# Two-block transformer kernel: compressed scores against zero-padded keys of two heads, and fewer, larger visits of small products between the dense ones

## The reference, cut to what matters

```python
# first block: the index score of query block i, over 8 index heads
s_h = jnp.einsum('bqhd,bsd->bqhs', iqb, ikf) * idx_scale            # 64-long dot products
score = jnp.einsum('bqh,bqhs->bqs', iwb * w_scale, jax.nn.relu(s_h))
...
# second block: keys and values are compressed, 31 blocks of 32 tokens each, for 2 groups of heads
def compress(t, pe, w1, w2):
    tb = t[:, blk] + pe[:, None, :]
    tb = jnp.moveaxis(tb, 3, 2).reshape(B, n_cmp, G, CMP_BLOCK * D)  # 2048 long
    return jax.nn.gelu(tb @ w1) @ w2                                 # w1: 2048 x 256, w2: 256 x 64
k_cmp = partial_rope(rms_norm(compress(kc, pe_k, w1_k, w2_k), k_gains[0]), cmp_end)
v_cmp = compress(vc, pe_v, w1_v, w2_v)
s_cmp = jnp.einsum('bsghd,bngd->bghsn', q, k_cmp)                    # compressed scores, 8 heads, 64 long
p_cmp = masked_softmax(s_cmp, cmp_end[None, :] <= pos[:, None])
```

## Time and profile before

| | |
|---|---|
| median of 3 runs | 1563.77 us (1563.75 to 1566.7) |
| the profiled execution, its own time | 1567.3 us |
| its span in the profile | 1565.5 us |
| PE (TensorE products) busy | 1540.6 us, 98% of the span, 8659 instructions |
| PEld (weight loads) busy | 1248.5 us, 80% |
| DVE busy | 875.1 us, 56% |
| ACT busy | 609.3 us, 39% |
| chain that ended last | 90% PE, 6% DVE, 2% ACT |

### The profile page before, as it was taken

One profiled execution on the slowest core, in us unless ns is written; L12 is line 12 of the kernel. 1 busy time (PEld: TensorE's weight loads), 2 busy tenths in 40 slices (PEclk: granted clock), 3 DMA queues, 4 the chain that ended last, 5 costly groups with the idle time before them and its releaser, 6 DMA issues.

```text
span 1565.5 us, 21012 instructions
## 1 busy us (share of the span) xinstructions
PE 1540.6 (98%) x8659; PEld 1248.5 (80%) x8659; DVE 875.1 (56%) x1589; ACT 609.3 (39%) x1046; POOL 46.1 (3%) x82
## 2 busy tenths in 40 slices
PE   7999999999999999999999999999999999999999
PEld 5777887778888888888888886777778888888887
DVE  5669786665366753322243575777466544655332
ACT  4443234642322532222232364665425433344320
POOL 1000000000000000000000011100010000000000
PEclk9999999999999999999999999999999999999999
DMA  9322112136344244222323133110113233222321
GB/s 371 145 74 102 54 68 81 55 133 237 128 148 175 95 175 161 95 94 81 108 95 104 44 113 134 55 42 15 55 60 129 81 108 108 95 91 84 121 67 54
DMA packets 44887, 165.83 MB, mean 106 GB/s; under 512 B 5108, under 2 KB 5236, under 8 KB 43640
## 3 DMA queue, kind: packets, MB, share of 16 engines
q1 hardware_dynamic: 44792, 164.50, 29.6%
HBM read 162.38 MB, written 2.10 MB: 105 GB/s over the span
## 4 chain that ended last, share of the span: by engine, by line
PE 90%; DVE 6%; ACT 2%; DMA 1%; issue 1%; SPq 0%; POOL 0%; DVEq 0%; ACTq 0%; POOLq 0%
PE bank L557 87%; PE bank L569 3%; DVE wl L1740 1%; ACT AR L1399 1%; DVE AR L1752 1%; DMA raw<-in_wst 1%; DVE AR L2062 0%; DVE G L1759 0%; ACT wh L1222 0%; DVE X L1752 0%; DVE Al L1752 0%; DVE CST L1752 0%; ACT AR L1407 0%; DVE ST L1752 0%; DVE PRMT L1752 0%
## 5 line engine op out<-in xcount | busy, mean ns | idle before, releaser
L1222 ACT ACTIVATE wh<-raw 128x1024 fp32r<-128x1024 f32 (+1 forms) x197 | 205.9, 1047 | 384.0 <-PE bank L557 372.7
L557 PE MATMUL bank<-wh,Hh 128*128 128x512 f32 (+1 forms) x784 | 318.3, 406 | 2.7 <-DVE Hl L1752 1.8
L1740 DVE TENSOR_TENSOR wl<-raw,wh 128x1024 fp32r<-128x1024 f32 (+1 forms) x197 | 236.4, 1208 | 137.8 <-ACT wh L1222 136.9
L557 PE MATMUL bank<-wh,Hl 128*128 128x512 f32 (+1 forms) x784 | 304.6, 389 | 0.0
L557 PE MATMUL bank<-wl,Hh 128*128 128x512 f32 (+1 forms) x784 | 303.8, 388 | 0.0
L557 PE MATMUL bank<-Hh,wh 128*128 128x512 f32 (+2 forms) x712 | 268.5, 377 | 0.2
L557 PE MATMUL bank<-Hl,wh 128*128 128x512 f32 (+2 forms) x712 | 266.9, 375 | 0.0
L557 PE MATMUL bank<-Hh,wl 128*128 128x512 f32 (+2 forms) x712 | 266.9, 375 | 0.0
L557 PEld LDWEIGHTS bank<-wh,Hh 128*128 128x128 f32 x784 | 148.0, 189 | 45.5 <-issue 18.5
L557 PEld LDWEIGHTS bank<-wh,Hl 128*128 128x128 f32 x784 | 147.7, 188 | 31.1
L557 PEld LDWEIGHTS bank<-wl,Hh 128*128 128x128 f32 x784 | 148.3, 189 | 25.7
(11 more groups left out here) (251 smaller groups left out, 1866.2 us busy)
## 6 DMA issues: line engine op xcount, KB each, us to landing
raw<-in_wst SPq DMA_DIRECT2D x268, 512.0 KB, 3.4
AR<-in_wst SPq DMA_DIRECT2D x8, 1024.0 KB, 11.2
X<-in_x SPq DMA_DIRECT2D x8, 512.0 KB, 5.2
AR<-in_wst SPq DMA_DIRECT2D x5, 512.0 KB, 6.1
out<-X SPq DMA_DIRECT2D x8, 256.0 KB, 2.1
CST<-in_cst SPq DMA_DIRECT2D x1, 1619.0 KB, 9.7
raw<-in_wst SPq DMA_DIRECT2D x4, 296.0 KB, 2.7
BC<-in_bc SPq DMA_DIRECT2D x2, 512.0 KB, 8.0
```

What stands on the lines that cost most here:

```text
L557: return e.matmul(o, l, r, start=start, stop=stop, skip_group_check=True)
L1222: e.activation(HI[slot[i]][:, 0:width(i)], raw[:, i % NR, 0:width(i)], ACT.Copy).then_inc(*w_hi.mark(i))
L1740: e.tensor_tensor(LO[slot[i]][:, 0:n], raw[:, i % NR, 0:n], HI[slot[i]][:, 0:n].bitcast(f32), SUB).then_inc(*w_lo.mark(i))
```

## The change

Five things change.

1. The first layer of the compression is done in 4 visits of four contraction tiles each, in place of 16 visits of one. The last visit is at the same tick as before.
2. Index scores of block 1 are done in 2 visits of two head pairs, those of block 3 in 3 visits (the last with two head pairs, using banks 6 and 7 as well). Block 2 keeps its 4 visits.
3. The compressed keys of a group are stored twice with zeros between (`KCB`, 128 x 128: keys of the group in rows 0 to 63 for one head, in rows 64 to 127 for the other, zeros elsewhere). One product with 128 rows of contraction and 64 columns then gives two heads' scores: 4 products per block in place of 8. They go to bank 2 in place of banks 4 and 5. The mask is added by one VectorE instruction in place of two.
4. VectorE's copy of the compressed keys out of bank 2 becomes two copies of 64 partitions and moves ahead of the maxima of the second attention's first unit. A memset for the zeros is added.
5. In both attentions ScalarE copies the finished value bank (`share`) between the two halves of the transposes' copies, in place of behind the exponentials.

```diff
+        def index_bank(i, hp, j):
+            return (4 + j + 2 * (i == hp == 3), 256 * (hp % 2) if i == 1 else 0)
...
-        kcT = W("gk", 64, 64).rearrange("p (g n) -> p g n", g=2)
+        KCB = W("gk", 64, 128)
+        kcB = KCB.rearrange("p (g c n) -> p g c n", g=2, c=2)
...
-                    for hp in range(4):
+                    for hps in {1: ((0, 1), (2, 3)), 2: ((0,), (1,), (2,), (3,)), 3: ((0,), (1,), (2, 3))}[i]:
...
-                        claim(4)
-                        claim(5)
-                        for j in (0, 1):
...
+                        for b in {index_bank(i, hp, j)[0] for hp in hps for j in (0, 1)}:
+                            claim(b)
+                        for hp in hps:
+                            for j in (0, 1):
...
+                                x = mm(bank[b][:, o:o + n], iqT[r, hp, tok(i)], ikT[r, 0:n], True, True)
...
             def compressed():
-                for _ in range(9):
+                for _ in range(8):
                     yield
                 for c in range(4):
+                    for _ in range(4):
+                        yield
                     on.wait_ge(s_cw[c % 3], 32 * (c // 3 + 1))
...
                         if q == 3:
                             x.then_inc(*small.mark(("comp", c)))
-                        yield
+                yield
...
                     on.wait_ge(*dve.of(("kc",)))
-                    claim(4)
-                    claim(5)
-                    for h in range(8):
-                        r = slice(64 * (h % 2), 64 * (h % 2) + 64)
-                        x = mm(bank[4 + h % 2][:, 32 * (h // 2):32 * (h // 2) + 32], qT[r, h // 2, tok(i)], kcT[r, h // 4, :], True, True)
+                    claim(2)
+                    for hp in range(4):
+                        x = mm(bank[2][:, 64 * hp:64 * hp + 64], qT[:, hp, tok(i)], KCB[:, 64 * (hp // 2):64 * (hp // 2) + 64], True, True)
                     x.then_inc(*small.mark(("cscore", i)))
-                    for par in (0, 1):
-                        free[4 + par] = dve.of(("cadd", i, par))
+                    free[2] = dve.of(("cadd", i))
...
                 for u in range(n + 3):
+                    ends = u >= 3 and a.ends(u - 3)
                     if 2 <= u < n + 2:
-                        for j in (0, 1):
-                            turn_part(u - 2, j)
+                        turn_part(u - 2, 0)
+                    if ends:
+                        i = a.units[u - 3][0]
+                        on.wait_ge(*small.of((a.tag, "close", i) if closed else (a.tag, "value", u - 3)))
+                        if i:
+                            on.wait_ge(*dve.of((a.tag, "out", i - 1)))
+                        e.activation(a.both, bank[a.vbanks[0]][:, :], ACT.Copy).then_inc(*act.mark((a.tag, "share", i)))
+                    if 2 <= u < n + 2:
+                        turn_part(u - 2, 1)
                     if u < n:
                         exps(u)
...
-                for _ in range(3):
-                    yield
+                on.wait_ge(*act.of(("kw", "T", 1)))
+                e.memset(KCB, 0.0).then_inc(*dve.mark())
+                yield
+                yield
                 on.wait_ge(*small.of(("kc",)))
-                copy(kcT, bank[2][:, 0:64].rearrange("p (g n) -> p g n", g=2), ("kc",))
+                own()
+                for c in (0, 1):
+                    r = slice(64 * c, 64 * c + 64)
+                    copy(kcB[r, :, c, :], bank[2][r, 0:64].rearrange("p (g n) -> p g n", g=2), *[("kc",)] * c)
+                yield
...
-                    for par in (0, 1):
-                        tt(pc.rearrange("p (j c n) -> p j c n", j=4, c=2)[:, :, par, :], bank[4 + par][:, 0:P].rearrange("p (j n) -> p j n", j=4),
-                           C("cadd", 32 * i, 32).unsqueeze(1).broadcast_to([P, 4, 32]), ADD, ("cadd", i, par))
+                    tt(p3, bank[2][:, 0:256].rearrange("p (h n) -> p h n", h=8), C("cadd", 32 * i, 32).unsqueeze(1).broadcast_to([P, 8, 32]), ADD, ("cadd", i))
```

More of the change, by code:

```diff
@@ L736, in index @@
                     n = (i + 1) * P
-                    for hp in range(4):
+                    for hps in {1: ((0, 1), (2, 3)), 2: ((0,), (1,), (2,), (3,)), 3: ((0,), (1,), (2, 3))}[i]:
                         on.wait_ge(*act.of(("iq", "T", i)))
                         on.wait_ge(*dve.of(("ik", "T")))
-                        claim(4)
-                        claim(5)
-                        for j in (0, 1):
[L743 to L746, removed]
-                        yield
-                        yield
-                        if i > 1:
+                        for b in {index_bank(i, hp, j)[0] for hp in hps for j in (0, 1)}:
+                            claim(b)
+                        for hp in hps:
+                            for j in (0, 1):
+                                r = half(j)
+                                b, o = index_bank(i, hp, j)
+                                x = mm(bank[b][:, o:o + n], iqT[r, hp, tok(i)], ikT[r, 0:n], True, True)
+                                x.then_inc(*small.mark(("index", i, 2 * hp + j)))
+                                free[b] = act.of(("relu", i, 2 * hp + j))
+                        for _ in hps:
                             yield
+                            yield
+                            if i > 1:
+                                yield
             w.beside(index())
@@ L1316, in index @@
                         m = 8 * (i - 1) + h
-                        on.wait_ge(*small.of(("index", i, h)))
+                        on.wait_ge(*small.of(("index", i, h | 2 if i == 1 else h)))
                         if m >= 2:
                             on.wait_ge(*dve.of(("score", m - 2)))
-                        e.activation(RL[m % 2][:, 0:n], bank[4 + h % 2][:, 0:n], ACT.Relu, scale=0.125).then_inc(*act.mark(("relu", i, h)))
+                        b, o = index_bank(i, h // 2, h % 2)
+                        e.activation(RL[m % 2][:, 0:n], bank[b][:, o:o + n], ACT.Relu, scale=0.125).then_inc(*act.mark(("relu", i, h)))
                         yield
@@ L1409, in attention @@
                 for u in range(n + 3):
+                    ends = u >= 3 and a.ends(u - 3)
                     if 2 <= u < n + 2:
-                        for j in (0, 1):
-                            turn_part(u - 2, j)
+                        turn_part(u - 2, 0)
[7 more added lines that the diff above has]
+                        turn_part(u - 2, 1)
                     if u < n:
                         exps(u)
-                    if u >= 3:
-                        i = a.units[u - 3][0]
-                        if a.ends(u - 3):
-                            on.wait_ge(*small.of((a.tag, "close", i) if closed else (a.tag, "value", u - 3)))
-                            if i:
-                                on.wait_ge(*dve.of((a.tag, "out", i - 1)))
-                            e.activation(a.both, bank[a.vbanks[0]][:, :], ACT.Copy).then_inc(*act.mark((a.tag, "share", i)))
-                            due.append(i)
-                        elif due:
-                            high(due.pop())
+                    if ends:
+                        due.append(i)
+                    elif due:
+                        high(due.pop())
                     yield
```

2 lines of the change are left out of this document (removed).

## The result

| | before | changed |
|---|---|---|
| median of 20 runs each, taken together | 1566.43 us | 1563.49 us |
| fastest and slowest of them | 1563.75 and 1568.31 | 1560.28 and 1565.44 |
| profiled execution, its span | 1565.5 us | 1559.0 us |
| mean granted clock in the profile | 0.996 | 0.999 |

The medians differ by 2.94 us. The ratio of the runs, compared with each other, is 0.9979, with an interval of 0.9972 to 0.9986, which is 3.3 us (2.2 to 4.4) of 1566.4. The kernel got faster, by about what can be told from no change. The forecast was 4.8 us and 1559.0 us. The measured median is 4.5 above that: 2.66 of it is the level from which I subtracted (1563.77 where 20 runs give 1566.43), and 1.86 is the difference of the medians, 2.94 in place of 4.8.

What follows compares the result with a forecast made beforehand. TensorE, busy 98% of the span, was taken as the bound. Savings of 2.2 + 0.4 + 0.6 + 0.1 + 1.2 + 0.9 - 0.6 = 4.8 us off the 1563.8 median gave 1559.0, range 1556.0 to 1563.8.

Steps and rivals of the forecast that it cites:

- The price of a visit: Compression and index scores: a visit costs 0.80 us, 0.38 of it for entering and leaving tiles, which merging saves.
- the tie at chunk 3: Before the hidden layer's transposes: TensorE comes 1.1 us early and waits for ScalarE's gelu, so 0.1 us is saved.
- Rival D: Compression and index scores: the surcharge belongs to each product, so grouping saves nothing; 1563.1 us, chance 0.04.
- `share` and the copy out of bank 2: First attention: ScalarE's earlier copy saves 0.9 us. Second attention: earlier VectorE copies remove TensorE's bank 2 wait, saving 1.5.
- rival A: Second attention, blocks 1 to 3: bank 2 waits bring half clocks; slower, 1565.3 to 1567.0 us, chance 0.07.
- Zeros against tiles: Compressed scores: eight whole-array records take 0.96 us against 1.23 for 16 in tiles; 0.27 saved per block, 1.1 together.
- Rival E: Compressed scores: products that are half zeros cost twice a packed pair, 4 x 1.0 us more; 1563.0 us, chance 0.05.
- The waits on bank 2: Compressed scores of blocks 1, 2, 3 wait 1.3, 3.8, 1.1 us for VectorE's copy; 3.2 lost net.
- The net of block 3: Second attention, block 3: a wait of 1.1 us comes, the 1.85 goes; 0.7 gained, besides the scores' 0.3.
- the clock: Second attention: one half-clock loss goes with the 1.85 us wait, one comes with the 3.8; nothing counted.
- Rival B: From 945 us on: ScalarE and VectorE ties leave only 1 to 2.5 us saved; 1561.3 to 1562.8, chance 0.22.
- C's cheaper case: Second attention: old half clock's 1.7 us goes, none follows new waits, cheaper whole-array product; 1556.7 us, chance 0.14 including 1557.3.

Runs made afterwards that it cites:

- e4_comp16: The changed kernel with the compression's first layer in 16 visits again; median 1566.15 us, ratio 0.9992 to the kernel before.
- e5_comp_last4: The changed kernel with only the compression's last chunk in four visits again; median 1562.04 us, ratio 0.9974 to the kernel before.
- e6_index12: The changed kernel with the index scores of blocks 1 and 3 in four visits each again; median 1563.74 us, ratio 0.9985.
- e7_share_late: The changed kernel with ScalarE's copy of the finished value bank behind the exponentials again, in both attentions; median 1566.55 us, ratio 1.0006.
- e8_copy_late: The changed kernel with VectorE's two copies of the compressed keys one visit later, behind the maxima; median 1563.96 us, ratio 0.9992.
- e3_tiles45: As e2_banks45, but the compressed scores are eight products in two row tiles of 64 again; median 1555.72 us, ratio 0.9930.
- e10_block2: The changed kernel with only block 2's scores one tick behind the transposes of block 1's probabilities; median 1562.53 us, ratio 0.9974.
- e1: The changed kernel with each next block's compressed scores one tick behind the transposes of the block's probabilities; median 1555.28 us, ratio 0.9927.
- e2_banks45: The changed kernel with the whole-array compressed scores back in banks 4 and 5, two mask additions; median 1554.49 us, ratio 0.9919.
- e9_best: e2_banks45 with the hidden layer's transposes one tick later and VectorE's mask addition ahead of its bank 2 copy; median 1554.78 us, ratio 0.9927.
- e11_two_chunks: e9_best with the compression's chunks 0 and 1 in one visit at chunk 1's place; median 1553.35 us, ratio 0.9921.

## Why the prediction was right and where it failed

**The price of a visit** held: eight steps in 1.88, a surcharge that goes once per merge. Chunks 0 and 1, the wait before them, chunk 2, the tie at chunk 3 and the index scores came to 2.96 + 1.34 against 3.3 + 1.2, and e4_comp16 (2.9 for the compression), e5_comp_last4 (the tie) and e6_index12 (1.3) bear them out. Chunk 2 was put 0.2 too high. Rival D falls.

**`share` and the copy out of bank 2** held: 1.2 and 2.1 to 0.9 and 1.8, by e7_share_late and e8_copy_late. That `share` is also what keeps block 3's wait at 1.2, the prediction had only as a part of rival A; e7_share_late shows it, with 3.5 us.

**Zeros against tiles:** 0.30 per block for 0.27, though a part of it ends in a wait. Rival E falls by e3_tiles45.

**The waits on bank 2** were foretold in place, cause and length. The net of block 3 was not: without the half clock it is -0.4 for 1.0, by a wait for the maxima among other things that the prediction did not have. The sum over all places, 4.3 for 4.8 with one half clock on either side, hides this: other places gave 0.9 more than forecast. That part is luck.

**The step that failed** is the one behind the waits, the clock. In the prediction's words: "I expect one such loss for the other and count nothing", and with it "So I take the 4.8 off the median: 1563.8 - 4.8 = 1559.0". In the two profiles it looks right, since one half clock of 3.4 us is in each behind 1000. In the timed runs it isn't. The kernel before ran 61 times beside the experiments. 19 of these runs had a mean clock of 1.0, no half clock at all (one of 3.4 us makes it 0.999), and took 1563.7 to 1565.0, with the median at 1564.2. The changed kernel had none in 20 runs; the four best had 0.999 and took 1560.3 to 1560.8. Of 49 runs of e4 to e8, which keep the wait of 3.74, none had a clock of 1.0, and of the ten of e10_block2, with waits of 2.37 and 2.88, one had. Of 22 runs of the five kernels without such a wait (e1, e2, e3, e9, e11), 12 had a clock of 1.0. In all seven profiles with a wait of 2.4 to 3.8 in block 2 (the changed kernel, e4 to e8, e10) there is a half clock of 3.4 to 6.8 us at that wait. So the new wait brings its 1.7 us or more practically each time, while the old one of 1.85 was without it in at least 19 of 61 runs. An estimate of what this took: the share of the clock that was not granted, times the span, is 2.9 us in the mean of the 61 runs before and 4.3 in the mean of the 20 changed ones. Not all of that is lost time, since a half clock within a wait costs nothing. By it, some 1.4 of the missing 1.9 went to the clock; the other 0.5 is what the places of the profiles fall short, 4.3 for 4.8.

The same step has the error of the level. The median of three from which I subtracted, 1563.8, is as low as only the runs without a half clock are, and most runs of the kernel before have one: 14 of the 20 took over 1565.0. That is 2.7 of the 4.5 by which the median was missed. The other figure in the prediction, 1562.5 from the profiled execution's own time, would have been off by 1.0.

Against runs of before without a half clock the change is worth 4.3 - 1.7 = 2.6 by the profiles, and 1564.2 - 1560.6 = 3.6 by the best runs. The difference of 1 is about as large as that between first dense products in different profiles of these kernels (0.1 to 1.4 late), and I leave it open.

Rival A had the mechanism that cost most of the missing gain, with a price of 2.4 for each half clock (measured: 1.7, and 2.6 to 3.2 in its long form, part of which lies in the wait and costs nothing), but placed it far outside the likely case, with a chance of 0.07. Its total, 1565.3 or more, did not come. Rival B, given back between 945 and 999, did not happen: nothing is lost there but the chunk 3 tie. C's cheaper case needed a run without the half clock, and the change's own wait excluded it.

The early half clock between 18 and 25 us is in the profiles of before, e2, e4 and e9 (the short form in e5 and e7) and in no other. None of the edits touches that place, so it comes and goes there without them; what decides it is not shown.

## What to carry to other kernels

A visit of small tiled products between dense ones pays a fixed price for going into the tiles and back. Merging visits saves it, until the merged visit meets an engine in a tie; read that tie from the waits before merging, and move its consumer one tick later (worth 1.2 in e9_best). A merge also moves the work behind it forward in the row, and e11_two_chunks shows that this can make a new tie.

Before a product is given a bank, look at what reads the bank last and what stands ahead of that reader on its own engine. Here the choice of one bank in place of two others was a loss of 6 us, 1.7 of it by the clock. And a long wait of TensorE has two prices, its length and the half clock at it; a median of three runs does not say whether the second one is in it. Look at the mean granted clock of each run before subtracting from a median.

## What the runs showed of the hardware that was not expected

TensorE's clock fell to half (1.2 GHz) at every one of nine waits of 2.37 to 3.76 us (seven profiles, blocks 2 and 3). It began between 1.4 us before the wait's end and 1.4 us after it. Where it began after the end it lasted 3.4 us (1.7 lost), where it began inside the wait 6.8 us (e5, e6, e8 and block 3 of e10; 2.6 to 3.2 lost in the first three). These are nine waits in seven executions; that one timed run of e10_block2 had a mean clock of 1.0 says that it is not without exception. Behind waits of up to 1.7 it never came between 900 and 1160; at 1.85 (before) it came and at 2.08 (e8_copy_late) it did not. The Trainium skill (TensorE: Matmul & The Clock Gate, HAM oscillation) says that pauses between bursts of work send the engine back to half clock. These rows agree, and here one pause between dense products was enough, of 2.4 to 3.8 us in nine places and of 1.85 us in one.

Whole-array products with half of their weights zero cost 0.81 in place for eight heads' scores (e2_banks45), where eight products in pairs of row tiles cost 1.01 (e3_tiles45). The Trainium skill (TensorEngine Tiling (Array Packing), Overview) has up to twice the speed for such pairs; with 32 columns each these runs show no gain from them.
